# The token rows of k: transposed on VectorE in 32 by 32 blocks and stored in 128-byte runs by ScalarE, in place of TensorE transposes and a GpSimd store

## The chip, the core and the metric

The kernel runs on one core of a Trainium2 chip. The metric is device time in microseconds (us) for one execution; lower is better. Engines are TensorE (PE in the rows, its weight loads PEld), VectorE (DVE), ScalarE (ACT), GpSimd (POOL) and SyncE (SP). A transfer is requested by an engine's sequencer (SPq, ACTq, POOLq) and carried by 16 DMA engines that all requesters share.

## The reference, cut to what matters

One decoder layer is run on a group of 256 prompt tokens and a group of 8 samples with 4 tokens each, 288 tokens together. What matters here is that k leaves the kernel twice: inside, for attention, and as an output of its own with one row of 16 heads by 64 numbers per token.

```
h = _rmsnorm(x, g_pre) * (1.0 + scale) + shift
q, k, v, f, u, bg, cg, ga, gb = _split_cols(h @ w_in, IN_SIZES)
...
kp_l.append(k); vp_l.append(v)      # prompt: (256, 16, 64)
...
ks_l.append(k); vs_l.append(v)      # samples: (8, 4, 16, 64)
```

All numbers are float32. Every big product is made of three passes (high part by high part, and two cross terms).

## The kernel before, in words

Activations are kept transposed: a tile such as `kT` has 128 features on the partitions and, for each of 8 feature tiles, 288 tokens side by side. A product takes one megabyte of weights (`raw`, a ring of 4 buffers that SyncE fills), which ScalarE rounds to `w_hi` (L1327, `split_hi`) and VectorE turns to the remainder `w_lo` (L1794, `split_lo`), each in 2 buffers. TensorE then runs 48 matmuls (L675 to L677), in four column blocks of 12, numbered `mt` 0 to 3. `w_hi` of product n can be made only when product n-2 is done, since it uses the same buffer.

The stage around the change is the projection to q, k and v: a loop of 24 products, `u` = 0 to 23. I call them product 0 to 23. Products 0 to 11 make the first half of the features (q, k, v by four products each), 12 to 23 the second half. So `kT` is complete after product 19. Each engine has its own program, written out by hand; work is placed in it behind `if u == ...`, and semaphores join the engines. Nothing reorders it.

The token rows of k are made so. `turn_rows` has TensorE transpose four 128 by 128 tiles of `kT` into a PSUM bank (L951), 6 times for k and 6 times for v; ScalarE and VectorE take turns to copy the bank out (`copy_row`, L438) into `k_rows`, and GpSimd requests two stores of them (L2733, L2734). On TensorE two of the six stand behind product 19 and four behind product 21. Behind product 20 stands `turn_suf` (L943), 16 transposes for the bias of the samples; it waits for `cum_done`, which VectorE gives at the end of `copy_sums` (its last copies are L2183), and for the first two k row copies.

Behind product 21 ScalarE copies the four banks of `turn_suf` (L1505) and signals `sufT_done`. In product 23, the last, TensorE also transposes pages of the key cache (`turn_k`, L972): two ahead of `mt` 1 and two ahead of `mt` 2. The second pair uses the same banks as the first, and waits until ScalarE (`copy_KT`, L1489) and VectorE have copied them out. Ahead of that copy ScalarE does `new_keys` (L1493). In attention, ScalarE's `pair_hi(0)` (L1569) writes where `k_rows` lay, so it waits until the stores of k have landed (`s_kout`).

Of the kernel before, what the change touches and what calls it, by code (L numbers as in the profile page):

```python
# [67 lines left out]
def layer(nc, x_prompt, x_sample, cache_k, cache_v, cache_logf, state_conv, page_table, c_prompt,  # L68
# [86 lines left out]
    LAST = KT - 1  # L155
    H_HI = KT // PIECE

    ROWS = ([("k", half, b) for half in range(2) for b in range(3)]
            + [("v", 0, 0), ("v", 0, 1), ("v", 1, 0), ("v", 1, 1), ("v", 0, 2), ("v", 1, 2)])
    ROW_BANK = (4, 5, 4, 5, 6, 7, 6, 7, 2, 3, 7, 2)  # L160
    KEYS = PAST + TS
    CT = KA // 2

# [1 line left out]
    with ctx:  # L165
# [7 lines left out]
        def place(name, shape, dt=F32, where=None):  # L173
# [99 lines left out]
        k_rows = place("k_rows", [P, 3, DA], where=R)  # L273
# [102 lines left out]
        fixed, newk_ready, pool_sel, sums_ready = (sem(n) for n in ("fixed", "newk_ready", "pool_sel", "sums_ready"))  # L376
        z_ready, z_ps, z_out = sem("z_ready"), sem("z_ps"), sem("z_out")
        y_made = sem("y_made")
        rowT_ps, rowT_a, rowT_d, suf_ps, suf_done, sufT_ps, sufT_done = (sem(n) for n in (
            "rowT_ps", "rowT_a", "rowT_d", "suf_ps", "suf_done", "sufT_ps", "sufT_done"))  # L380

# [44 lines left out]
        def row_tile(n):  # L426

            name, half, b = ROWS[n]
            at_ = slice(512 * half, 512 * half + 512)
            if name == "k":  # L430
                return k_rows[0:min(P, NT - b * P), b, at_]
            return v_rows[half][:, b, :] if b < 2 else v_new[:, at_]

        def copy_row(eng, copy, n):
# [221 lines left out]
        def _(pe):  # L656
# [289 lines left out]
            def turn_rows(n):  # L946

                name, half, b = ROWS[n]
                rows = min(P, NT - b * P)
                for j in range(4):  # L950
                    mm = pe.transpose(bank[ROW_BANK[n]][0:rows, j * P:j * P + P],  # L951
                                      (kT if name == "k" else vT)[:, 4 * half + j, b * P:b * P + rows], ident[:, :])
                mm.then_inc(rowT_ps, 1)

            def turn_k(s, ns):
# [20 lines left out]
            def first_rows(mt):  # L976

                if mt == 1:
                    pe.wait_ge(rowT_a, 3)
                    pe.wait_ge(rowT_d, 3)  # L980
                    turn_k(0, (0, 1))
                if mt == 2:
                    turn_k(0, (2, 3))
                if mt == 3:
                    pe.wait_ge(bank_turn, BT + MT * (G_QKV + 4))
                    turn_rows(6)
                    turn_rows(7)

            for u in range(QKV):
                t = u % PER_HALF  # L990
                product(N_QKV + u, t % 4 == 0, t % 4 == 3, G_QKV + u // 4, SK * (t % 4), a_hi, a_lo, u % SPLIT,
                        None, first_rows if u == QKV - 1 else None)
                if u in ADA_AT:
                    v = 1 + ADA_AT.index(u)
                    pe.wait_ge(ada_turned, v)
                    ada_rows(v % SK, use=A_B1 + v + 1 - SPARE)
                if u == 0:
                    turn_z()
                if u == 3:
                    turn_lf()  # L1000
                if u == 19:
                    sums_of_lf()
                    pe.wait_ge(ada_turned, 1 + len(ADA_AT))
                    pe.wait_ge(ada_mods, A_B1 + 1)
                    pe.wait_ge(bank_turn, BT + MT * (G_QKV + 3))
                    turn_rows(0)
                    turn_rows(1)
                if u == 20:
                    turn_suf()
                if u == 21:  # L1010
                    pe.wait_ge(sufT_done, 1)
                    pe.wait_ge(bank_turn, BT + MT * (G_QKV + 6))
                    for n in range(2, 6):
                        turn_rows(n)

            def scores(s):

# [101 lines left out]
            scores(0)  # L1119
            pe.wait_ge(pool_sel, 1)  # L1120
            pe.wait_ge(sufT_done, 1)
            pe.wait_ge(rowT_a, 4)
            sample_scores(0)
            pe.wait_ge(bank_turn, BT + MT * (G_MIX + 1))
            turn_rows(8)
            turn_rows(9)
            pe.wait_ge(rowT_d, 4)
            turn_rows(10)
            pe.wait_ge(rowT_a, 5)
            turn_rows(11)  # L1130
            turn_k(1, (0, 1))
            scores(1)
            pe.wait_ge(rowT_a, 6)
            pe.wait_ge(rowT_d, 6)
            turn_p(0, 0)
            turn_p(0, 1)
            turn_k(1, (2, 3))
# [181 lines left out]
        def _(act):  # L1319
# [172 lines left out]
            def new_keys(j):  # L1492
                nc.scalar.copy(KTs[j][:, :, PAST:KEYS], kT[:, :, TP:NT]).then_inc(sK_new, 1)  # L1493

            for u in range(QKV):
                n = N_QKV + u
                if u < QKV - 1:
                    split_hi(n + 1, (u + 1) % RAW, (n + 1) // RAW + 1, (u + 1) % SPLIT)
                if u == 20:
                    copy_row(act, nc.scalar.copy, 0)  # L1500
                if u == 21:
                    act.wait_ge(sufT_ps, 1)
                    act.wait_ge(fixed, 1)
                    for b in range(4):
                        ins = nc.scalar.copy(bias_s[:, 2 * b:2 * b + 2, 0:PAST],  # L1505
                                             bank[4 + b][:, :].rearrange("p (s n) -> p s n", s=2))
                    ins.then_inc(sufT_done, 1)
                if u == 22:
                    copy_row(act, nc.scalar.copy, 2)
                    copy_row(act, nc.scalar.copy, 4)  # L1510
                if u == QKV - 1:
                    groups_done(N_QKV + u - 1, MT - 1)
                    new_keys(0)
                    copy_KT(0, 0)
                    evict(u, 0)
                    copy_KT(0, 2)
                    evict(u, 1)
                    copy_row(act, nc.scalar.copy, 6)
# [46 lines left out]
            def pair_hi(s):  # L1565
                act.wait_ge(O_ps, s + 1)
                if s == 0:
                    act.wait_ge(s_kout, 32)
                nc.scalar.copy(o_hi[:, s, 0:TP], bank[3][:, 0:TP]).then_inc(O_hi, 1)  # L1569

            def sample_hi(s):
# [6 lines left out]
                ins.then_inc(sO_hi, 1)  # L1578

            exp_head(0, 0)  # L1580
            copy_row(act, nc.scalar.copy, 8)
            copy_row(act, nc.scalar.copy, 10)
            exp_head(0, 1)
            exp_sample(0)
            act.wait_ge(rowT_ps, len(ROWS))
# [202 lines left out]
        def _(dve):  # L1788
# [398 lines left out]
            def copy_KT(s, n):  # L2187
# [54 lines left out]
            copy_row(dve, nc.vector.tensor_copy, 7)  # L2242

            def max_head(s, j):

# [55 lines left out]
            max_head(0, 0)  # L2301
            max_head(0, 1)
            max_sample(0)
            copy_row(dve, nc.vector.tensor_copy, 9)
            norm_head(0, 0)
            copy_row(dve, nc.vector.tensor_copy, 11)
            copy_KT(1, 1)
            norm_head(0, 1)
            max_head(1, 0)
# [336 lines left out]
        def _(pool):  # L2646
# [81 lines left out]

            pool.wait_ge(bank_turn, BT + MT * (G_QKV + 5))
            samples_q(0)  # L2730
            pool.wait_ge(rowT_a, 3)
# [3 lines left out]
            samples_q(1)  # L2735
            pool.wait_ge(rowT_a, 6)
            pool.wait_ge(rowT_d, 6)
# [11 lines left out]
            pool.wait_ge(s_kout, 32)  # L2749
            pool.wait_ge(s_zout, 32)  # L2750


# [56 lines left out]
```

## Time and profile before

| | us |
|---|---|
| median of 3 runs | 1783.26 (1783.14 to 1783.98) |
| the profiled execution | 1783.0 |
| its span in the trace | 1781.4 |
| TensorE busy in the span | 1768.5 |
| VectorE busy | 911.0 |
| ScalarE busy | 693.8 |
| the stage of this change (product 19's end to product 23's end) | 377.8 to 412.8 |

The profiled execution took 1.6 us more than its span; what lies around the span is not touched by the change. Times in the rows are us from the start of the span. Matmul rows overlap each other by their pipeline, so their start times tell the pace, not their durations.

### The profile page before, as it was taken

The page shows a single profiled execution, that of the slowest core. Times are in us where ns is not written, and L with a number is a line of the kernel's source. Part 1 is how long each engine was busy: PE and PEld are TensorE (multiplying, and loading weights), DVE is VectorE, ACT ScalarE, POOL GpSimd, SP SyncE. Part 2 cuts the span into 40 slices and gives each one's busy share as a digit, 9 for nine tenths or more (in the row PEclk, how much of TensorE's full clock was granted, in tenths as well). Part 3 has the DMA queues.
Part 4 walks back from the last instruction along what each step waited for, and adds up shares of the span by engine and source line. Part 5 has one row for each costly group of instructions (what it writes and reads, how often), then busy time and mean ns, then how long its engine had stood idle before and what let it go on. Part 6 is the DMA issues. An engine that isn't in the chain of part 4 may idle for free.

```text
span 1781.4 us, 31779 instructions
## 1 busy us (share of the span) xinstructions
PE 1768.5 (99%) x13592; PEld 1664.2 (93%) x13592; DVE 911.0 (51%) x1137; ACT 693.8 (39%) x809; POOL 26.1 (1%) x76
## 2 busy tenths in 40 slices
PE   8999999999999999999999999999999999999999
PEld 6888888897699999998979999999999999999998
DVE  4666663245644344455686444434443445566565
ACT  5332232235643333343354233333333334445454
POOL 0000100001000000000000000000000000000000
PEclk9999999999999999999999999999999999999999
DMA  9988578856754444458866444444444444444441
GB/s 380 409 333 336 214 309 343 355 200 223 262 185 165 163 159 167 162 196 343 332 245 265 142 166 165 165 165 165 165 165 165 165 163 166 164 163 164 163 161 71
DMA packets 59234, 382.38 MB, mean 215 GB/s; under 512 B 6912, under 2 KB 7728, under 8 KB 17026
## 3 DMA queue, kind: packets, MB, share of 16 engines
q1 hardware_dynamic: 57632, 378.27, 56.0%
q0 software_dynamic: 1328, 2.58, 0.4%
q8 instruction: 74, 1.21, 0.3%
q14 instruction: 22, 0.18, 0.0%
q10 hardware_dynamic: 178, 0.13, 0.0%
HBM read 376.15 MB, written 4.81 MB: 214 GB/s over the span
## 4 chain that ended last, share of the span: by engine, by line
PE 96%; DMA 1%; DVE 1%; ACT 1%; issue 1%; SPq 0%; DVEq 0%; ACTq 0%
PE bank L675 29%; PE bank L677 29%; PE bank L676 28%; PE bank L695 3%; PE bank L685 1%; PE bank L972 1%; DMA ada<-in_w_ada 1%; PE bank L1102 1%; PE bank L1071 0%; PE bank L1290 0%; DMA ada_o<-in_w_ada 0%; PE bank L1041 0%; PE bank L951 0%; PE bank L1051 0%; PE bank L898 0%
## 5 line engine op out<-in xcount | busy, mean ns | idle before, releaser
L675 PE MATMUL bank<-a_lo,w_hi 128*128 128x288 f32 x3624 | 1077.0, 297 | 1.4 <-DVE a_lo L1978 0.7
L676 PE MATMUL bank<-a_hi,w_hi 128*128 128x288 f32 x3624 | 1069.1, 295 | 0.0
L677 PE MATMUL bank<-a_hi,w_lo 128*128 128x288 f32 x3624 | 1065.5, 294 | 0.0
L1794 DVE TENSOR_TENSOR w_lo<-raw,w_hi 128x2048 fp32r<-128x2048 f32 x239 | 547.9, 2292 | 699.9 <-ACT w_hi L1327 699.2
L1327 ACT CAST w_hi<-raw 128x2048 fp32r<-128x2048 f32 x238 | 453.9, 1907 | 850.2 <-PE bank L677 824.7
L675 PEld LDWEIGHTS bank<-a_lo,w_hi 128*128 128x128 f32 x3624 | 678.9, 187 | 20.7 <-issue 19.2
L677 PEld LDWEIGHTS bank<-a_hi,w_lo 128*128 128x128 f32 x3624 | 682.6, 188 | 0.0
L676 PEld LDWEIGHTS bank<-a_hi,w_hi 128*128 128x128 f32 x3624 | 680.3, 188 | 0.0
L1906 DVE TENSOR_TENSOR a_lo<-hid,a_hi 128x1152 fp32r<-128x1152 f32 x44 | 59.4, 1351 | 12.3 <-ACT a_hi L1351 12.3
L1351 ACT CAST a_hi<-hid 128x1152 fp32r<-128x1152 f32 x44 | 50.7, 1154 | 0.0
L675 PE MATMUL bank<-o_lo,w_hi 128*128 128x288 f32 x128 | 37.9, 296 | 0.0
L675 PE MATMUL bank<-y_lo,w_hi 128*128 128x288 f32 x128 | 37.9, 296 | 0.0
L676 PE MATMUL bank<-o_hi,w_hi 128*128 128x288 f32 x128 | 37.8, 295 | 0.0
L676 PE MATMUL bank<-y_hi,w_hi 128*128 128x288 f32 x128 | 37.8, 295 | 0.0
L677 PE MATMUL bank<-o_hi,w_lo 128*128 128x288 f32 x128 | 37.6, 294 | 0.0
L677 PE MATMUL bank<-y_hi,w_lo 128*128 128x288 f32 x128 | 37.6, 294 | 0.0
L695 PE MATMUL bank<-ada,cT 128*32 128x512 f32 x288 | 32.8, 595 | 0.0
L1743 ACT ACTIVATE sg<-bank 128x288 f32<-128x288 f32 x44 | 18.0, 408 | 36.9 <-PE bank L677 36.9
L685 PE MATMUL bank<-ada,cT 128*32 128x512 f32 (+1 forms) x320 | 30.9, 512 | 0.6 <-DMA ada<-in_w_ada 0.6
L2578 DVE TENSOR_TENSOR sg<-bank,sg 128x288 f32<-128x288 f32 x44 | 19.0, 454 | 15.4 <-ACT sg L1743 15.4
L1663 ACT ACTIVATE sq<-bank 128x288 f32<-128x288 f32 x32 | 13.1, 409 | 32.5 <-PE bank L677 32.5
L695 PEld LDWEIGHTS bank<-ada,cT 128*32 128x32 f32 x288 | 8.4, 109 | 17.6 <-issue 17.6
(387 smaller groups left out, 973.4 us busy)
## 6 DMA issues: line engine op xcount, KB each, us to landing
raw<-in_w_ffn_in SPq DMA_DIRECT2D x88, 1024.0 KB, 4.8
raw<-in_w_in SPq DMA_DIRECT2D x75, 1024.0 KB, 7.9
ada<-in_w_ada SPq DMA_DIRECT2D x60, 1024.0 KB, 8.9
raw<-in_w_ffn_out SPq DMA_DIRECT2D x44, 1024.0 KB, 4.8
ada_o<-in_w_ada SPq DMA_DIRECT2D x24, 1024.0 KB, 8.4
raw<-in_w_o SPq DMA_DIRECT2D x16, 1024.0 KB, 4.9
ada<-in_w_ada SPq DMA_DIRECT2D x16, 512.0 KB, 12.6
raw<-in_cache_k SPq DMA_DIRECT2D x16, 512.0 KB, 4.2
```

The costliest lines, as they stand in the source:

```text
L675: pe.matmul(acc, w_hi[buf][:, a, cols], lo[:, kt, :], start=first and a == 0, stop=False)
L676: pe.matmul(acc, w_hi[buf][:, a, cols], hi[:, kt, :], start=False, stop=False)
L677: mm = pe.matmul(acc, w_lo[buf][:, a, cols], hi[:, kt, :], start=False, stop=last and a == tiles - 1)
L685: mm = pe.matmul(bank[4][32 * a:32 * a + 32, 0:src.shape[2]], cT[:, SK * q + a, :], src[:, a, :], start=q == 0, stop=q == SK - 1, tile_pos ...
L695: mm = pe.matmul(bank[4][32 * a:32 * a + 32, :], cT[:, k, :], ring[q][:, a, :], start=first and q == 0, stop=last and q == SK - 1, tile_po ...
L972: mm = pe.transpose(bank[4 + n % 2][:, f * P:f * P + P], raw[2 * j][:, n, f * P:f * P + P], ident[:, :])
L1327: nc.scalar.copy(w_hi[buf][:, :, :], raw[s][:, :, :]).then_inc(hi_done, 1)
L1351: nc.scalar.copy(dst[:, kd:kd + tiles, :], src[:, bass.ds(kt, tiles), :]).then_inc(act_hi, 1)
L1743: nc.scalar.activation(sg[:, mt, :], bank[mt][:, 0:NT], ACT.Sigmoid).then_inc(gate_done, 1)
L1794: tt(w_lo[buf][:, :, :], raw[s][:, :, :], w_hi[buf][:, :, :].bitcast(F32), ALU.subtract).then_inc(raw_turn, 1)
L1906: tt(lo[:, kd:kd + SK, :], src[:, bass.ds(kt, SK), :], hi[:, kd:kd + SK, :].bitcast(F32), ALU.subtract).then_inc(act_lo, 1)
L2578: tt(sg[:, mt, :], bank[mt][:, 0:NT], sg[:, mt, :], ALU.mult).then_inc(bank_turn, 1)
```

## The change

K's rows no longer pass through TensorE and PSUM. VectorE transposes `kT` in blocks of 32 by 32 from SBUF to SBUF, one instruction of 128 partitions by 1152 elements for each half of the features, into `k_blocks` (which lies where `k_rows` lay). In a block the tokens are now on 32 partitions and 32 features lie side by side, so a store writes runs of 32 numbers, 128 bytes. ScalarE requests the stores: for each half 16 of 32 partitions by 8 runs (the prompt) and 4 of 32 partitions by 4 runs (the samples), 20 requests; 40 in all. In the output each run stands alone, so there are 32 times 256 runs for the prompt and 8 times 128 for the samples, 9216. `turn_rows` and `copy_row` remain for v, with new numbers, and GpSimd keeps the stores of v.

```diff
-    ROWS = ([("k", half, b) for half in range(2) for b in range(3)]
-            + [("v", 0, 0), ...])
+    ROWS = ([("v", 0, 0), ("v", 0, 1), ("v", 1, 0), ("v", 1, 1), ("v", 0, 2), ("v", 1, 2)])
+    K_STORES = 4 * (KA + 2)
...
             def turn_suf():
                 pe.wait_ge(suf_done, 1)
                 pe.wait_ge(cum_done, 1)
-                pe.wait_ge(rowT_a, 1)
-                pe.wait_ge(rowT_d, 1)
+                pe.wait_ge(ada_turned, 1 + len(ADA_AT))
...
                 if mt == 1:
-                    pe.wait_ge(rowT_a, 3)
-                    pe.wait_ge(rowT_d, 3)
+                    pe.wait_ge(sufT_done, 1)
                     turn_k(0, (0, 1))
...
                 if u == 19:
                     sums_of_lf()
-                    turn_rows(0)
-                    turn_rows(1)
                 if u == 20:
                     turn_suf()
-                if u == 21:
-                    for n in range(2, 6):
-                        turn_rows(n)
...
+            def store_k(half):
+                tiles = slice(KA // 2 * half, KA // 2 * half + KA // 2)
+                prompt = k_prompt[0, 0].rearrange("(j r) (k x) (y c) -> x y r k j c", r=32, x=2, y=2)
+                sample = k_sample[0].rearrange("s t (k x) (y c) -> x y (s t) k c", x=2, y=2)
+                act.wait_ge(k_turned, half + 1)
+                for i in range(4):
+                    rows = slice(32 * i, 32 * i + 32)
+                    for k in range(KA // 2 * half, KA // 2 * half + KA // 2):
+                        act.dma_start(prompt[i // 2, i % 2, :, k, :, :],
+                                      k_blocks[rows, k, 0:TP].rearrange("p (j c) -> p j c", c=32)).then_inc(s_kout, 16)
+                    act.dma_start(sample[i // 2, i % 2, :, tiles, :], k_blocks[rows, tiles, TP:NT]).then_inc(s_kout, 16)
...
-                if u == 20:
-                    copy_row(act, nc.scalar.copy, 0)
                 if u == 21:
                     act.wait_ge(sufT_ps, 1)
...
                     ins.then_inc(sufT_done, 1)
+                    store_k(0)
                 if u == 22:
-                    copy_row(act, nc.scalar.copy, 2)
-                    copy_row(act, nc.scalar.copy, 4)
+                    store_k(1)
...
             def pair_hi(s):
                 act.wait_ge(O_ps, s + 1)
                 if s == 0:
-                    act.wait_ge(s_kout, 32)
+                    act.wait_ge(s_kout, 16 * K_STORES)
...
+            def turn_k_blocks(half):
+                dve.wait_ge(bank_turn, BT + MT * (G_QKV + 3 + 3 * half))
+                tiles = slice(KA // 2 * half, KA // 2 * half + KA // 2)
+                nc.vector.transpose(k_blocks[:, tiles, :].rearrange("p k n -> p (k n)"),
+                                    kT[:, tiles, :].rearrange("p k n -> p (k n)")).then_inc(k_turned, 1)
...
                 if u == 20:
                     copy_sums()
-                    copy_row(dve, nc.vector.tensor_copy, 1)
-                if u == 22:
-                    copy_row(dve, nc.vector.tensor_copy, 3)
-                    copy_row(dve, nc.vector.tensor_copy, 5)
+                    turn_k_blocks(0)
+                if u == 21:
+                    turn_k_blocks(1)
...
-            pool.dma_start(k_prompt[0, 0].rearrange("(b p) h d -> p b (h d)", p=P), k_rows[:, 0:2, :]).then_inc(s_kout, 16)
-            pool.dma_start(k_sample[0].rearrange("s t h d -> (s t) (h d)"), k_rows[0:TS, 2, :]).then_inc(s_kout, 16)
```

On ScalarE, from the `w_hi` of product 22 (the first row) to the first page copy of product 23, the program before reads:

```order
L1327 CAST w_hi_78<-raw_76 128x2048
L1505 COPY bias_s<-bank 128x2x256 x4
L1327 CAST w_hi_80<-raw_77 128x2048
L438 COPY k_rows<-bank 32x512
L438 COPY k_rows<-bank 128x512
L1493 COPY KTs_132<-kT 128x8x32
L1489 COPY KTs_132<-bank 128x4x128
```

The same stretch of ScalarE's program in the changed kernel, where the line numbers have shifted and each pair of rows of DMA requests is one quarter of a half:

```order
L1314 CAST w_hi_78<-raw_76 128x2048
L1503 COPY bias_s<-bank 128x2x256 x4
L1491 DMA out<-k_blocks 32x8x32 x4
L1493 DMA out<-k_blocks 32x4x32
...
L1314 CAST w_hi_80<-raw_77 128x2048
L1491 DMA out<-k_blocks 32x8x32 x4
L1493 DMA out<-k_blocks 32x4x32
...
L1480 COPY KTs_132<-kT 128x8x32
L1476 COPY KTs_132<-bank 128x4x128
```

The pair of request rows stands four times in each place: 20 requests now stand between the bias copies and the `w_hi` of product 23, and 20 between that and the page copy; two row copies have gone.

On VectorE, from the last copies of `copy_sums` to the page copies of product 23, the program before reads:

```order
L2183 COPY bias_s<-bank 128x4 x8
L438 COPY k_rows<-bank 128x512
L1794 TENSOR_TENSOR w_lo_79<-raw_76,w_hi_78 128x2048
L1794 TENSOR_TENSOR w_lo_81<-raw_77,w_hi_80 128x2048
L438 COPY k_rows<-bank 128x512
L438 COPY k_rows<-bank 32x512
L2197 COPY KTs_132<-bank 128x4x128 x2
```

And in the changed kernel:

```order
L2181 COPY bias_s<-bank 128x4 x8
L2202 STREAM_TRANSPOSE k_blocks<-kT 128x1152
L1792 TENSOR_TENSOR w_lo_79<-raw_76,w_hi_78 128x2048
L2202 STREAM_TRANSPOSE k_blocks<-kT 128x1152
L1792 TENSOR_TENSOR w_lo_81<-raw_77,w_hi_80 128x2048
L2195 COPY KTs_132<-bank 128x4x128 x2
```

One transpose now stands ahead of the `w_lo` of product 22 and one behind it; three row copies have gone.

## Rows read from the trace of the kernel before

**Rows 1.** The page: busy time by engine, and the chain by engine.

```profile
PE 1768.5 (99%) x13592; PEld 1664.2 (93%) x13592; DVE 911.0 (51%) x1137; ACT 693.8 (39%) x809; POOL 26.1 (1%) x76
...
PE 96%; DMA 1%; DVE 1%; ACT 1%; issue 1%; SPq 0%; DVEq 0%; ACTq 0%
```

**Rows 2.** Instructions of line 951: engine, operation, count, duration ns min/median/max.

```profile
L951 PE MATMUL bank<-ident,kT x24: 271/272/329, 379.6 to 397.3; 128*128 128x128 f32 x16, 128*32 128x128 f32 x8
```

**Rows 3.** Timeline of TensorE: start us, us, instruction, idle before and releaser.

```profile
387.46 1.94 PE L943 MATMUL bank<-ident,suf 128*128 128x128 f32 x16 [0.39 <-DVE k_rows L438]
...
395.63 1.91 PE L951 MATMUL bank<-ident,kT 128*32 128x128 f32 x16
397.30 0.38 PE L675 MATMUL bank<-a_lo,w_hi 128*128 128x288 f32 x1
```

**Rows 4.** Timeline of VectorE, products 20 to 22.

```profile
385.82 0.64 DVE L2183 COPY bias_s<-bank 128x4 f32<-128x4 f32 x8
386.62 0.69 DVE L438 COPY k_rows<-bank 128x512 f32<-128x512 f32 x1 [0.16 <-DVE bias_s L2183]
...
397.82 2.29 DVE L1794 TENSOR_TENSOR w_lo<-raw,w_hi 128x2048 fp32r<-128x2048 f32 x1 [6.43 <-ACT w_hi L1327]
```

**Rows 5.** Timeline of ScalarE, products 21 to 23.

```profile
387.16 1.90 ACT L1327 CAST w_hi<-raw 128x2048 fp32r<-128x2048 f32 x1 [6.30 <-PE bank L677]
389.44 2.05 ACT L1505 COPY bias_s<-bank 128x512 f32<-128x512 f32 x4 [0.37 <-PE bank L943]
395.88 1.90 ACT L1327 CAST w_hi<-raw 128x2048 fp32r<-128x2048 f32 x1 [4.39 <-PE bank L677]
...
403.97 0.41 ACT L1493 COPY KTs<-kT 128x256 f32<-128x256 f32 x1 [5.23 <-PE bank L677]
406.01 0.59 ACT L1489 COPY KTs<-bank 128x512 f32<-128x512 f32 x1 [1.63 <-PE bank L972]
```

**Rows 6.** Timeline of TensorE: product 23's start and its second pair of page transposes.

```profile
403.77 0.30 PE L675 MATMUL bank<-a_lo,w_hi 128*128 128x288 f32 x1
...
407.85 1.03 PE L972 MATMUL bank<-ident,raw 128*128 128x128 f32 x8
```

**Rows 7.** Instructions of tile ada_sb: VectorE's transpose of 128 by 512 out of PSUM.

```profile
L1886 DVE STREAM_TRANSPOSE ada_sb<-bank x14: 707/709/717, 199.4 to 1004.9; 128x512 f32<-128x512 f32 x14
```

**Rows 8.** Timeline of ScalarE and its queue: the three requests that it makes.

```profile
172.31 1.91 ACT L1327 CAST w_hi<-raw 128x2048 fp32r<-128x2048 f32 x1 [4.49 <-PE bank L677]
172.32 0.40 ACTq L1459 DMA_DIRECT2D bf<-in_b_f  x1
172.75 0.53 ACTq L1460 DMA_DIRECT2D table<-in_page_table  x1
173.31 0.36 ACTq L1461 DMA_DIRECT2D wf<-in_w_f  x1
```

**Rows 9.** Instructions of line 470: SyncE's weight requests, duration ns min/median/max.

```profile
L470 SPq DMA_DIRECT2D raw<-in_w_in x75: 327/333/1079, 42.1 to 741.9; - x75
```

**Rows 10.** Windows: busy us and count by engine, TensorE clock, DMA share, GB/s.

```profile
10.00:20.00 10.00, 9.46 (x96) 6.49 (x98) 4.56 (x17) 5.45 (x12) 0.00 (x0) 1.00 1.03 414
...
1775.00:1777.00 2.00, 2.00 (x21) 2.00 (x20) 1.88 (x4) 1.30 (x3) 0.00 (x0) 1.00 1.02 366
...
391.00:409.00 18.00, 18.00 (x143) 17.88 (x143) 4.64 (x6) 5.15 (x10) 1.25 (x2) 1.00 0.50 183
```

**Rows 11.** The page: ScalarE's DMA queue, packets, MB, share of 16 engines.

```profile
q10 hardware_dynamic: 178, 0.13, 0.0%
```

**Rows 12.** Timeline of ScalarE: the copy that waits for the landed k stores.

```profile
422.21 0.35 ACT L1569 CAST o_hi<-bank 128x256 fp32r<-128x256 f32 x1
```

**Rows 13.** Timeline of SyncE's queue: a request near the start, and key pages of sample 1.

```profile
9.37 1.75 SPq L499 DMA_DIRECT2D raw<-in_w_in  x1
...
391.56 0.85 SPq L579 DMA_DIRECT2D raw<-in_cache_k  x2
```

**Rows 14.** The chain in order of time: transposes of the key pages of sample 1.

```profile
417.31 0.87 PE bank L972 x8
```

More of the change, by code:

```diff
@@ L156, in layer @@
     H_HI = KT // PIECE
-    ROWS = ([("k", half, b) for half in range(2) for b in range(3)]
-            + [("v", 0, 0), ("v", 0, 1), ("v", 1, 0), ("v", 1, 1), ("v", 0, 2), ("v", 1, 2)])
-    ROW_BANK = (4, 5, 4, 5, 6, 7, 6, 7, 2, 3, 7, 2)
+    ROWS = ([("v", 0, 0), ("v", 0, 1), ("v", 1, 0), ("v", 1, 1), ("v", 0, 2), ("v", 1, 2)])
+    ROW_BANK = (6, 7, 2, 3, 7, 2)
+    K_STORES = 4 * (KA + 2)
     KEYS = PAST + TS
@@ L272, in layer @@
         o_lo = place("o_lo", [P, KA, NT], F32R, where=R + B_ACT8)
-        k_rows = place("k_rows", [P, 3, DA], where=R)
+        k_blocks = place("k_blocks", [P, KA, NT], where=R)
         upto = place("upto", [P, TP], where=R + 3 * DA * 4)
@@ L378, in layer @@
         y_made = sem("y_made")
+        k_turned = sem("k_turned")
         rowT_ps, rowT_a, rowT_d, suf_ps, suf_done, sufT_ps, sufT_done = (sem(n) for n in (
@@ L429, in row_tile @@
             at_ = slice(512 * half, 512 * half + 512)
-            if name == "k":
-                return k_rows[0:min(P, NT - b * P), b, at_]
             return v_rows[half][:, b, :] if b < 2 else v_new[:, at_]
@@ L951, in turn_rows @@
                     mm = pe.transpose(bank[ROW_BANK[n]][0:rows, j * P:j * P + P],
-                                      (kT if name == "k" else vT)[:, 4 * half + j, b * P:b * P + rows], ident[:, :])
+                                      vT[:, 4 * half + j, b * P:b * P + rows], ident[:, :])
                 mm.then_inc(rowT_ps, 1)
@@ L985, in first_rows @@
                     pe.wait_ge(bank_turn, BT + MT * (G_QKV + 4))
-                    turn_rows(6)
-                    turn_rows(7)
+                    turn_rows(0)
+                    turn_rows(1)
             for u in range(QKV):
@@ L1121, in _ @@
             pe.wait_ge(sufT_done, 1)
-            pe.wait_ge(rowT_a, 4)
+            pe.wait_ge(rowT_a, 1)
             sample_scores(0)
             pe.wait_ge(bank_turn, BT + MT * (G_MIX + 1))
[L1125 to L1130, printed above, removed]
+            turn_rows(2)
+            turn_rows(3)
+            pe.wait_ge(rowT_d, 1)
+            turn_rows(4)
+            pe.wait_ge(rowT_a, 2)
+            turn_rows(5)
             turn_k(1, (0, 1))
             scores(1)
-            pe.wait_ge(rowT_a, 6)
-            pe.wait_ge(rowT_d, 6)
+            pe.wait_ge(rowT_a, 3)
+            pe.wait_ge(rowT_d, 3)
             turn_p(0, 0)
@@ L1517, in _ @@
                     evict(u, 1)
-                    copy_row(act, nc.scalar.copy, 6)
+                    copy_row(act, nc.scalar.copy, 0)
                     evict(u, 2)
@@ L1580, in _ @@
             exp_head(0, 0)
-            copy_row(act, nc.scalar.copy, 8)
-            copy_row(act, nc.scalar.copy, 10)
+            copy_row(act, nc.scalar.copy, 2)
+            copy_row(act, nc.scalar.copy, 4)
             exp_head(0, 1)
@@ L2235, in _ @@
                     copy_sums()
-                    copy_row(dve, nc.vector.tensor_copy, 1)
-                if u == 22:
-                    copy_row(dve, nc.vector.tensor_copy, 3)
-                    copy_row(dve, nc.vector.tensor_copy, 5)
+                    turn_k_blocks(0)
+                if u == 21:
+                    turn_k_blocks(1)
             copy_KT(0, 1)
             copy_KT(0, 3)
-            copy_row(dve, nc.vector.tensor_copy, 7)
+            copy_row(dve, nc.vector.tensor_copy, 1)
             def max_head(s, j):
@@ L2303, in _ @@
             max_sample(0)
-            copy_row(dve, nc.vector.tensor_copy, 9)
+            copy_row(dve, nc.vector.tensor_copy, 3)
             norm_head(0, 0)
-            copy_row(dve, nc.vector.tensor_copy, 11)
+            copy_row(dve, nc.vector.tensor_copy, 5)
             copy_KT(1, 1)
@@ L2730, in _ @@
             samples_q(0)
+            samples_q(1)
             pool.wait_ge(rowT_a, 3)
             pool.wait_ge(rowT_d, 3)
-            pool.dma_start(k_prompt[0, 0].rearrange("(b p) h d -> p b (h d)", p=P), k_rows[:, 0:2, :]).then_inc(s_kout, 16)
-            pool.dma_start(k_sample[0].rearrange("s t h d -> (s t) (h d)"), k_rows[0:TS, 2, :]).then_inc(s_kout, 16)
-            samples_q(1)
-            pool.wait_ge(rowT_a, 6)
-            pool.wait_ge(rowT_d, 6)
             for half in range(2):
@@ L2748, in _ @@
             pool.wait_ge(s_out, 16 * 6)
-            pool.wait_ge(s_kout, 32)
+            pool.wait_ge(s_kout, 16 * K_STORES)
             pool.wait_ge(s_zout, 32)
```

5 lines of the change are left out of this document (removed).

## The prediction

> **What bounds the kernel now.** I read the page first. TensorE is busy for 1768.5 of 1781.4 us and holds 96% of the chain that ended last [rows 1]. So time is saved only by what leaves TensorE's own sequence, and lost by whatever makes TensorE wait. Next I read the timelines of the three compute engines around the change, to see who waits for whom there. TensorE runs without a gap, except for 0.39 us ahead of the transposes of `turn_suf`, where it waits for VectorE's k row copy [rows 3]. ScalarE is idle most of this stage: 4.39 us ahead of the `w_hi` of product 23 and 5.23 us ahead of `new_keys` [rows 5]. The change spends those two gaps.
>
> **What TensorE sheds.** 24 transposes leave [rows 2]. Eight stood behind product 19; taking them away only lets product 20 end sooner, and then `turn_suf` waits for VectorE. It started at 387.46, 0.15 us after the k row copy (386.62 + 0.69 = 387.31) [rows 3, 4]. Without that copy it follows the end of `copy_sums`, 385.82 + 0.64 = 386.46, by a signal and the same 0.15, some 386.7: **0.76 us sooner**. The other sixteen filled 395.63 to 397.30 [rows 3]: **1.67 us**, and some 0.1 for the slower first matmul behind a transpose (0.38 against 0.30) [rows 3, 6]. Together TensorE can gain at most 2.5 us. Undisturbed, product 21 would end at 395.63 - 0.76 = 394.87, product 23 would start at 403.77 - 2.5 = 401.27, and its second page transposes, in the trace at 407.85 [rows 6], would start at 405.35. I use this start as the mark: behind it TensorE's program is as before, so what the mark moves, the end moves.
>
> **What VectorE takes on.** Two transposes of 1152 elements. The nearest row is 709 ns for 512 elements out of PSUM [rows 7]; in proportion 1.6 us each. The first starts at about 386.6, ends at 388.2, and stands ahead of the `w_lo` of product 22. That one cannot start before its `w_hi`, which in the trace ends at 387.16 + 1.90 = 389.06 [rows 5]; with product 20 ending up to 0.9 sooner, 388.2. So the first costs nothing, and product 22 needs its `w_lo` only at 394.87. The second runs in VectorE's idle 6.43 us ahead of the `w_lo` of product 23 [rows 4]. If the transpose cost twice as much, 3.2 us, `w_lo` of product 22 would end at 389.8 + 2.3 = 392.1, still in time. Cost 0. The row copies that leave both engines were in gaps too.
>
> **What ScalarE takes on.** This decides. A sequencer makes requests one after the other, and each one behind them waits. Let c be the time from one request to the next. The nearest rows are ScalarE's own three requests: 0.40, 0.53 and 0.36 us, and from 172.32 to 173.67 the three take 1.35 us, so c = 0.45 [rows 8]. SyncE's repeated requests have 0.333 us at the median [rows 9], with the 0.03 us between neighbours c = 0.36. Upward, one request of the group at the start took 1.75 us [rows 13], which I come to below. I take 0.45: it is the same queue. The same rows show that requests run while the cast that stands ahead of them (172.31, 1.91 us) is still under way, so the casts and copies ahead do not add to them.
>
> - The bias copies start 0.76 sooner, at 388.68, and the last of the four is begun some 1.5 us later, at 390.2. There the first 20 requests start, and `k_turned` has come by then. They end at 390.2 + 20c = 399.2.
> - Only then can the `w_hi` of product 23 start, in the trace at 395.88. From its start to the end of `w_lo` are 397.82 + 2.29 - 395.88 = 4.23 us [rows 4, 5]. Product 23 can start at 394.5 + 20c = 403.5, not at 401.27: TensorE stands 2.2 us. The mark, 4.08 us behind that start [rows 6], would be 398.6 + 20c = 407.6.
> - The next 20 requests run beside the cast and end at 390.2 + 40c = 408.2. Behind them wait `new_keys` (0.3 until the next) and the page copy (0.59) [rows 5], on which TensorE's second page transposes wait. So the mark cannot be sooner than 391.15 + 40c = **409.15**.
>
> The later of the two counts, the second for every c over 0.373. The mark moves by 409.15 - 407.85 = **+1.3 us**; in general by 40c - 16.7. Every 0.01 us of a request is worth 0.4 us of the kernel. With c = 0.36 the first bound holds, 398.6 + 7.2 = 405.8, and the kernel is 2.05 us faster; with c = 0.53, the longest of the three, it is 4.5 us slower.
>
> **Free, with its cover.** The landing: `pair_hi(0)` is at 422.21 [rows 12] and needs all stores; with the last request at 408.2 it has 14 us, more by the shift. The page loads: those of sample 1 are requested at 391.56 [rows 13] and used at 417.31 [rows 14], 25 us. GpSimd loses two requests that nobody waits for.
>
> **The runs of 128 bytes.** Each DMA engine gets 16 + 1 runs of a prompt store (256 over 16, and the signal) and 8 + 1 of a sample store: 32 x 17 + 8 x 9 = 616 in all. Let t be the time of one. Rows of 8 KB went at 414 GB/s [rows 10], 317 ns per row and engine; the output rows of 2 KB at 366 GB/s, 90 ns. A straight line through both gives 14 ns for a row and 4.7 for 128 bytes, so t = 18.5 ns as a lower estimate; it was read off far larger rows. The upper bound is ScalarE's queue itself: its share rounds to 0.0%, so under 0.05% of 16 x 1781.4 us, 14 us for 178 packets, 80 ns each [rows 11]. The DMA engines were busy 50% of 391 to 409, with the store of k in it (1.15 MB at the 366 GB/s, 3.2 us of 18); so loads take 32% and 68% is free. 616 x 18.5 ns = 11.4 us, over 0.68 = 16.8 us, just under the 18 us that 40 requests take. I take it as hidden, from the nearest figure, but by little.
>
> That a full queue holds its requester up is what the 1.75 us request shows: it was made at 9.37, when the DMA engines were at their full rate [rows 10, 13], and a neighbour without that load takes 0.33.
>
> A rule speaks against the change. The Trainium skill, "DMA: Bandwidth & Descriptors", section Specifications, says that a transfer needs 512 bytes or more for full rate and that below this a read-modify-write is done. No row of this trace shows stores of single short runs, so it neither agrees nor differs; by the rule the stores would come out as the third rival below, by the straight line as hidden.
>
> **The rivals.** *All is covered* (chance 0.10): requests cost what SyncE's repeated ones cost, c = 0.36 or less. For it: all 32 prompt requests have one shape and tensor. Against: ScalarE's own rows. -2 to -2.5 us, 1780.5 to 1781.
>
> *The queue fills* (0.23): t is 25 to 40 ns, and ScalarE can request only as fast as the runs drain. Leaving out some 60 runs per engine that may still stand in the queue at the end (an estimate: ahead of the slow request at 9.37 some six requests of 9 packets were open), the requests end at 390.2 + 556t/0.68, that is 20 us after for t = 25 and 33 for t = 40, and the mark moves by +4 to +16 us: 1787 to 1799. It takes over from the count of requests at t = 22 ns and passes 0.2% at 25, near the estimate.
>
> *Short runs are stored in two passes* (0.13): a run is first read and then written, and costs near the upper bound, 60 to 80 ns. 556 x 60 / 0.68 = 49 us and 65 us; the mark at 440 and 457, +32 to +48 us, 1815 to 1831. Against it: 80 is a bound, not a reading. This is the mechanism of the page's rule; its 512 bytes twice, at the straight line's 33 ns each, would be an estimate of 66 ns and 1820.
>
> *The requests themselves are dearer* (0.10): with three dimensions and 256 runs, twice the runs of any in the trace, c = 0.53 to 0.60. +4.5 to +7.3 us, 1787.5 to 1790.3. For it: the spread of 0.36 to 0.53 between simple ones.
>
> That the transposes do not leave is excluded by the order of the programs. A gain over 0.2% would need more than the 2.5 us that TensorE sheds; I leave 0.02 for what I overlook.
>
> **The numbers.** The profiled execution took 1783.0, its span 1781.4; the median of the runs is 1783.26. Forecast (chance 0.42): 1783.0 + 1.3 = 1784.3, its own range 1781 to 1786.6. What a measurement can tell from no change is 0.2%, 3.6 us. Same: 0.42 + 0.10 = 0.52. Slower: 0.23 + 0.13 + 0.10 = 0.46. Faster 0.02. The range reaches from all covered, 1780.5, to the upper end of the filled queue, 1799, and leaves out the two passes and some of the rest, under 2 in 10.
>
> **What would show it.** Right: 40 request rows of ScalarE's queue of about 0.42 us each; the second L972 of product 23 (L970 now) at about 409, with its idle time put down to ScalarE's page copy; product 23 starting at about 403.5 after 2 us of idle; `turn_suf` at 386.7; two VectorE transposes of 1.2 to 1.6 us. Wrong: requests that start at 0.4 and grow to 0.6 or more after the first few (the queue fills), or a `pair_hi(0)` that waits for a DMA. If the requests have 0.33 the gain of TensorE is kept. The forecast is wrong at once if c is over 0.507, where +3.6 us is passed.

## The result, and the profile after

The changed kernel took 1786.88 us (median of 18 runs, 1785.60 to 1788.68), the kernel before 1783.30 us on the same chip (18 runs, of which one took 9829 us; without that one the median is 1783.26). The ratio is 1.002, with a 95% interval of 1.0014 to 1.0026: 3.6 us slower. The forecast was 1784.3, with a range of 1780.5 to 1799. So the sign was right and the time lies in the range, but the loss is 2.6 us larger than the sum, which gave 1.0 to the median, and the time is 0.3 us above the range of 1781 to 1786.6 that belonged to this sum alone. The profiled execution took 1788.5 us, the second longest of its 18. Its stage also began 1.41 us later than in the trace of before, ahead of anything that the change touches. The last matmul that both programs share ahead of it (`bank<-upto,lfr`) starts at 378.83 in before and at 380.24 here (near the start of the trace TensorE waited 1.4 us for `in_x_sample` and 1.2 us for `ada_o`, against 0.2 and 0.7 before). I therefore take 1.41 from each time of after before I set it beside [rows 3 to 6].

The page of the changed kernel: busy times, the queue of ScalarE, the shares of the chain that ended last, and the largest group of TensorE, whose last column is its idle time and what ended it.

```profile
PE 1769.7 (99%) x13568; PEld 1665.5 (93%) x13568; DVE 911.6 (51%) x1136; ACT 692.3 (39%) x806; POOL 24.9 (1%) x74
...
q10 hardware_dynamic: 10034, 1.31, 0.4%
...
PE 96%; ACT 1%; DVE 1%; DMA 1%; ACTq 1%; issue 0%; SPq 0%; DVEq 0%
...
L674 PE MATMUL bank<-a_lo,w_hi 128*128 128x288 f32 x3624 | 1078.1, 297 | 4.4 <-DVE w_lo L1792 3.0
```

TensorE is busy 1.2 us *more* than before [rows 1], though 24 transposes left it. ACTq, ScalarE's requests, now stands in the chain with 1%. And one wait of 3.0 us for `w_lo` is new.

ScalarE's timeline in the stage, which answers to [rows 5]; ACTq rows are requests, a row with x4 holds four in sequence:

```profile
390.00 0.59 ACT L1503 COPY bias_s<-bank 128x512 f32<-128x512 f32 x1 [0.36 <-PE bank L941]
390.02 0.86 ACTq L1491 DMA_DIRECT2D out<-k_blocks  x2
...
390.90 1.51 ACTq L1491 DMA_DIRECT2D out<-k_blocks  x1
...
396.43 1.99 ACTq L1491 DMA_DIRECT2D out<-k_blocks  x4
...
400.94 0.47 ACTq L1493 DMA_DIRECT2D out<-k_blocks  x1
401.51 1.91 ACT L1314 CAST w_hi<-raw 128x2048 fp32r<-128x2048 f32 x1 [9.45 <-PE bank L676]
401.53 1.87 ACTq L1491 DMA_DIRECT2D out<-k_blocks  x4
...
411.33 0.47 ACTq L1493 DMA_DIRECT2D out<-k_blocks  x1
411.84 0.41 ACT L1480 COPY KTs<-kT 128x256 f32<-128x256 f32 x1 [8.43 <-issue]
412.15 0.58 ACT L1476 COPY KTs<-bank 128x512 f32<-128x512 f32 x1
```

The first 20 requests run from 390.02 to 401.41, and the cast of product 23 starts only behind them. The profile writes its idle time to TensorE (`PE bank L676`). The requests beside the gap show what it is: ScalarE's own sequencer was making requests throughout. The second 20 run beside the cast, to 411.80, and behind them stand `new_keys` (L1480) and the page copy (L1476).

TensorE's timeline behind product 22, which answers to [rows 6]:

```profile
405.79 0.61 PE L674 MATMUL bank<-a_lo,w_hi 128*128 128x288 f32 x1 [3.03 <-DVE w_lo L1792]
406.20 0.44 PE L675 MATMUL bank<-a_hi,w_hi 128*128 128x288 f32 x1
406.44 0.44 PE L676 MATMUL bank<-a_hi,w_lo 128*128 128x288 f32 x1
...
408.84 1.91 PE L970 MATMUL bank<-ident,raw 128*128 128x128 f32 x8
...
412.08 0.29 PE L676 MATMUL bank<-a_hi,w_lo 128*128 128x288 f32 x1
412.21 0.29 PE L674 MATMUL bank<-a_lo,w_hi 128*128 128x288 f32 x1
```

The windows of TensorE over the same stretch (length, busy time and count, granted clock, DMA share, GB/s):

```profile
400.00:402.00 2.00, 2.00 (x17) 1.00 0.41 66
402.00:404.00 2.00, 0.76 (x6) 1.00 0.37 58
404.00:406.00 2.00, 0.21 (x1) 0.69 0.37 58
406.00:408.00 2.00, 2.00 (x9) 0.50 0.66 112
408.00:410.00 2.00, 2.00 (x11) 0.50 0.98 377
```

Behind the idle 3.03 us the matmuls start 0.24 us apart in place of 0.13, and the granted clock is 0.50, that is 1.2 GHz. Such a slow engine counts as fully busy: from the shared matmul to the mark TensorE is busy 29.12 us where it was 28.63, +0.5 us in spite of the 2.5 us that left it. The other 0.7 us of the 1.2 lie ahead of the shared matmul and have nothing to do with the change. The mark, the second page transposes, starts at 412.79. Counted from the shared matmul that is 32.55 us, against 407.85 - 378.83 = 29.02 before: +3.53 us. That is nearly all of the difference of the medians, 3.58. (The two profiled executions lie 5.5 us apart: 1.41 ahead of the shared matmul, 3.53 here, and 0.56 behind the mark.) It starts just behind ScalarE's page copy (412.15 + 0.58 = 412.73).

### The profile page after: what moved, and what is told of

It reads as the page before. It is cut to its first block, busy times and chain, and to the rows that moved or that the text cites. A ratio compares the mean times of both kernels' runs of the same rounds, so it can differ in the third digit from the quotient of the medians.

```text
span 1786.9 us, 31761 instructions
## 1 busy us (share of the span) xinstructions
PE 1769.7 (99%) x13568; PEld 1665.5 (93%) x13568; DVE 911.6 (51%) x1136; ACT 692.3 (39%) x806; POOL 24.9 (1%) x74
## 3 DMA queue, kind: packets, MB, share of 16 engines
q10 hardware_dynamic: 10034, 1.31, 0.4%
## 4 chain that ended last, share of the span: by engine, by line
PE 96%; ACT 1%; DVE 1%; DMA 1%; ACTq 1%; issue 0%; SPq 0%; DVEq 0%
PE bank L674 29%; PE bank L676 28%; PE bank L675 28%; PE bank L694 3%; PE bank L684 2%; PE bank L970 1%; PE bank L1089 1%; PE bank L1058 0%; ACTq L1491 0%; DMA ada_o<-in_w_ada 0%; PE bank L1277 0%; DMA xs_rows<-in_x_sample 0%; PE bank L1028 0%; PE bank L731 0%; DVE w_lo L1792 0%
## 5 line engine op out<-in xcount | busy, mean ns | idle before, releaser
L676 PE MATMUL bank<-a_hi,w_lo 128*128 128x288 f32 x3624 | 1066.2, 294 | 0.0
L676 PEld LDWEIGHTS bank<-a_hi,w_lo 128*128 128x128 f32 x3624 | 683.3, 189 | 0.0
L676 PE MATMUL bank<-o_hi,w_lo 128*128 128x288 f32 x128 | 37.6, 294 | 0.0
L676 PE MATMUL bank<-y_hi,w_lo 128*128 128x288 f32 x128 | 37.6, 294 | 0.0
```

Source lines behind the costliest of these rows:

```text
L676: mm = pe.matmul(acc, w_lo[buf][:, a, cols], hi[:, kt, :], start=False, stop=last and a == tiles - 1)
```

## The experiments

Each experiment is an edit of the changed kernel. Medians are set against runs of the kernel before on the same chip: 1783.22 for the first four, 1782.95 for the other four. "The mark" is always counted from the same shared matmul, so +3.53 is that of the change.

**No stores.** What does TensorE gain when nobody makes the requests?

```diff
-                    store_k(0)
-                if u == 22:
-                    store_k(1)
...
-                    act.wait_ge(s_kout, 16 * K_STORES)
+                    act.wait_ge(k_turned, 2)
...
-            pool.wait_ge(s_kout, 16 * K_STORES)
```

> The changed kernel without any store of k (k_prompt and k_sample are left unwritten; VectorE still makes the blocks). Theory 1, requests: ScalarE's 40 requests are the whole loss, and without them only what TensorE shed is left: 2.5 us under the kernel before, 1780.8 us, the second pair of page transposes 2.5 us sooner than in the kernel before, and no idle time of TensorE between products 22 and 23. Rival: part of the 3.6 us comes from something else in the change (VectorE's transposes, GpSimd's order, the added waits); then this kernel stays above 1781.5.

Measured: 1780.31 us, ratio 0.9987 (0.9978 to 0.9996), 2.9 us faster; the mark moved by -2.59. So the removed transposes give what the sum said, 2.5 within 0.1, and VectorE's transposes cost nothing. The change loses all of that and 3.6 us more by its stores alone.

**Runs of 1 KB.** The same 32 prompt requests with the same bytes, but each writes 32 long runs in place of 256 short ones.

```diff
-                        act.dma_start(prompt[i // 2, i % 2, :, k, :, :],
-                                      k_blocks[rows, k, 0:TP].rearrange("p (j c) -> p j c", c=32)).then_inc(s_kout, 16)
+                        act.dma_start(wide[i, k, :, :], k_blocks[rows, k, 0:TP]).then_inc(s_kout, 16)
```

> The changed kernel with the 32 prompt requests storing 1 KB runs (2 per engine and request instead of 16) at wrong places of k_prompt; same number of requests, same bytes. Theory 1, the request itself costs about 0.47 to 0.5 us whatever its runs: the 40 requests still take 20 us, and the kernel stays at +2 to +4 us against the kernel before. Theory 2, the queue of short runs holds the requests up (one took 1.51 us in the changed kernel): the requests fall to 0.36 to 0.42 us, none is longer than 0.6, and the kernel is at -1.5 to +0.5 us.

Measured: 1785.11 us, ratio 1.0011 (1.0002 to 1.0020), 1.9 us slower than before, just under the first theory's +2 to +4; mark +1.58. The prompt requests of the changed kernel, then those of this one (minimum, median and maximum in ns, first and last start):

```profile
L1491 ACTq DMA_DIRECT2D out<-k_blocks x32: 356/473/1506, 390.0 to 410.8; - x32
```

```profile
L1491 ACTq DMA_DIRECT2D out<-k_blocks x32: 339/444/1115, 390.3 to 409.1; - x32
```

With an eighth of the runs the median request falls by only 0.03 us and the 40 together from 21.8 to 19.9 us. So most of the price belongs to the request itself, not to its runs. Of the 1.9 us between them 0.03 x 40 = 1.2 are the shorter requests and 0.4 the one long request. TensorE's two waits here, and three windows of the kernel:

```profile
404.95 0.40 PE L674 MATMUL bank<-a_lo,w_hi 128*128 128x288 f32 x1 [1.87 <-DVE w_lo L1791]
411.16 1.09 PE L970 MATMUL bank<-ident,raw 128*128 128x128 f32 x8 [1.88 <-ACT KTs L1476]
```

```profile
400.00:402.00 2.00, 2.00 (x18) 1.00 0.24 57
404.00:406.00 2.00, 1.05 (x8) 1.00 0.28 68
412.00:414.00 2.00, 2.00 (x18) 1.00 0.29 63
```

After 1.87 us of idle the clock stayed at 1.00 (the second window), and after the next 1.88 us too (the third). With it TensorE is early enough to be seen waiting for ScalarE's page copy, the bound that the sum named. In the changed kernel the slow clock covers that wait.

The windows also price the short runs for the DMA engines. They are busy 0.41 of the time at 66 GB/s with runs of 128 bytes, 0.24 at 57 GB/s with 1 KB. The Trainium skill ("DMA: Bandwidth & Descriptors", section Specifications) wants 512 bytes for full rate and has a read-modify-write below that. The trace agrees that short runs cost more for each byte, 1.5 times by these two windows. It does not show the 60 to 80 ns per run that the prediction's rival of two passes needed: ScalarE's queue was 0.4% busy, 0.004 x 16 x 1786.9 = 114 us over 10034 packets, some 11 ns each (10 to 13 by the rounding).

**Half by SyncE.** ScalarE keeps the first 20 requests, SyncE takes the second 20. This takes the page copy out from behind requests and leaves the delayed cast.

```diff
+            load_pages(1, 0)
+            store_k(1, sp)
+            load_pages(1, 1)
...
-                if u == 22:
-                    store_k(1)
```

> The changed kernel with the first 20 requests by ScalarE as before and the second 20 by SyncE, behind its request for the key pages of sample 1. Now ScalarE's page copy is free, and only the late w_hi of product 23 is left: product 23 starts about 0.6 us later than in the kernel before, behind 3 us of idle. Theory A, the idle costs its own length and no more: second page transposes 4.08 us behind that start, +0.6 us, 1783.9. Theory B, TensorE comes out of the idle at half its clock, as the changed kernel's rows show (0.24 us per matmul instead of 0.133), and the price is the slow stretch too: +2.5 to +3.5 us, hardly better than the changed kernel.

Measured: 1786.32 us, ratio 1.0019 (1.0010 to 1.0028), 3.1 us slower; mark +2.60. TensorE's row of product 23, and its windows:

```profile
404.44 0.40 PE L689 MATMUL bank<-a_lo,w_hi 128*128 128x288 f32 x1 [3.35 <-DVE w_lo L1805]
...
405.34 0.45 PE L690 MATMUL bank<-a_hi,w_hi 128*128 128x288 f32 x1
```

```profile
404.00:406.00 2.00, 1.56 (x7) 0.69 0.19 45
406.00:408.00 2.00, 2.00 (x11) 0.50 0.92 367
```

Nothing of ScalarE stands ahead of the mark now, and yet little is won. From the start of product 23 to the mark it is 10.19 - 4.44 = 5.75 us where it was 4.08 at full clock [rows 6]: the slow clock costs 1.7 us here. So the change is held by two bounds that lie near each other, ScalarE's second 20 requests and TensorE's own slow stretch, and taking the first away alone gives only 3.53 - 2.60 = 0.9 us of mark.

**All by SyncE.** The same with both halves, behind the request of the first pages of sample 1.

```diff
+            load_pages(1, 0)
+            store_k(0, sp)
+            store_k(1, sp)
+            load_pages(1, 1)
```

> All 40 requests by SyncE, behind its request for the key pages of sample 1 and ahead of those for the value pages of sample 1; ScalarE makes none. Theory 1, who requests is what costs: 2.5 us under the kernel before, 1780.8 us, as without stores. Theory 2, the short runs or the later page requests hold something up (the requests take about 18 us, so the value pages come 10 us later than before): the gain is smaller than without stores, by what TensorE or pair_hi(0) waits for a DMA; 1782 to 1786.

Measured: 1780.32 us, ratio 0.9989 (0.9980 to 0.9998), 2.9 us faster by the medians and 2.0 by the ratio; mark -2.58, as without any store. The requests as SyncE's queue made them:

```profile
L591 SPq DMA_DIRECT2D out<-k_blocks x32: 316/450/487, 391.3 to 411.8; - x32
```

They cost SyncE nearly what they cost ScalarE, 0.45 us, and up to the mark they cost the kernel nothing. Behind them wait the page loads. The value pages of sample 1 are requested at 414.0 and nobody waits for them, but the key pages of sample 2 follow at 416.25. That is 37.7 us behind the shared matmul, against 27.6 in the kernel without stores, whose row is this:

```profile
406.13 14.32 SPq L578 DMA_DIRECT2D raw<-in_cache_k  x4
```

Here TensorE stands for these pages, and the clock falls behind that wait:

```profile
416.25 4.29 SPq L578 DMA_DIRECT2D raw<-in_cache_k  x4
...
426.43 1.09 PE L986 MATMUL bank<-ident,raw 128*128 128x128 f32 x8 [2.22 <-DMA raw<-in_cache_k]
```

```profile
428.00:430.00 2.00, 2.00 (x10) 0.50 0.84 342
```

From the mark to a matmul behind this place (the fourth `bank<-ncum,pick` behind the mark, at 432.88) it is 27.90 us, against 24.15 without stores (404.92 to 429.07): 3.75 us lost, 2.22 of them by standing and 1.5 behind it. This profiled execution took 1783.93 us, the longest of eleven. The eleven fall into two groups, six of 1779.54 to 1780.32 us and five of 1782.23 to 1783.93 us, while all eleven without stores stay under 1781.5. So the second theory holds in at least one execution: the median of 1780.32 is that of the executions without the loss, and SyncE is not a free place for these requests. Only one execution was profiled, so that the other four lost their time to the same wait is likely but not shown.

**The clock kept up.** To the half-by-SyncE kernel I add dummy matmuls in the idle stretch of TensorE, ahead of product 23. They wait for `sufT_done`, that is until ScalarE has copied the banks of `turn_suf`. That was long ago when product 22 ends, so they begin right behind it.

```diff
+                if u == 22:
+                    pe.wait_ge(sufT_done, 1)
+                    keep_warm(6, bank[7])
```

> e3_half_by_act with six dummy matmuls (128 by 128 by 256, into a free bank, some 0.46 us each, together 2.8 us) on TensorE between products 22 and 23, where it stood idle for 3.35 us. Theory B of e3 (the idle halves TensorE's clock and the slow stretch is most of the price): the clock stays at 1.00, matmuls keep 0.133 us, the second page transposes start 4.08 us behind product 23, 2 us sooner than in e3: 1784.0 to 1784.6. Rival (the slow pace comes from the DMA traffic or from something else in that stretch): it stays at 1786.3.

Measured: 1784.42 us, ratio 1.0007 (0.9998 to 1.0016), 1.5 us over before in place of 3.1; mark +0.76 in place of +2.60.

```profile
401.13 2.75 PE L728 MATMUL bank<-ones 128*128 128x256 f32 x12
...
404.38 0.40 PE L689 MATMUL bank<-a_lo,w_hi 128*128 128x288 f32 x1 [0.49 <-DVE w_lo L1808]
```

```profile
406.00:408.00 2.00, 2.00 (x18) 1.00 0.96 363
```

Product 23 starts nearly where it does in the kernel without them (0.27 us sooner from the shared matmul), but at granted clock 1.00, and from there to the mark it is 408.56 - 404.38 = 4.18 us in place of 5.75. So the clock's price is 1.6 us. The medians give 3.10 - 1.47 = 1.6 too, but each of them is known to 1.6 us only, so it is the traces that show it. The DMA engines move as much in the window of 406 to 408 as without the dummies (363 and 367 GB/s), so the traffic does not make the slow pace.

**The clock kept up in the changed kernel.** The same lines in the changed kernel itself.

> The changed kernel with the same six dummy matmuls. Here ScalarE's page copy behind all 40 requests holds the second page transposes as well, until about the same moment as the slow clock did. So the clock stays at 1.00 and nothing is gained, or at most 0.3 us: 1786.5 to 1787; TensorE's slow stretch turns into a wait for the page copy of some 2 to 3 us. Rival: the slow clock is what set the time, and the kernel gains 1.5 us or more.

Measured: 1788.08 us (7 runs), ratio 1.0027 (1.0016 to 1.0039), 5.1 us over before; the mark +3.57, where the change has it. I had expected no change of time, and it became 1.5 us slower. TensorE's rows, and its windows:

```profile
403.83 0.40 PE L674 MATMUL bank<-a_lo,w_hi 128*128 128x288 f32 x1 [0.16 <-DVE w_lo L1795]
...
411.16 1.55 PE L970 MATMUL bank<-ident,raw 128*128 128x128 f32 x8 [3.00 <-ACT KTs L1479]
412.75 0.44 PE L675 MATMUL bank<-a_hi,w_hi 128*128 128x288 f32 x1
```

```profile
410.00:412.00 2.00, 0.84 (x6) 0.91 0.16 26
412.00:414.00 2.00, 2.00 (x11) 0.50 0.11 29
```

The mark is held by ScalarE, as expected. But the fast product 23 now arrives 3.00 us early and waits there, the clock falls *behind* the mark, and there nothing covers the slow matmuls: from the mark to the fourth `bank<-ncum,pick` it is 25.77 us (411.16 to 436.93), against 24.22 in the changed kernel (412.79 to 437.01), 1.55 us more. In the changed kernel the slow stretch lay in time that TensorE would have waited anyway.

**Second half by ScalarE.** The mirror of the third experiment: SyncE makes the first 20 requests, ScalarE the second.

```diff
+            load_pages(1, 0)
+            store_k(0, sp)
+            load_pages(1, 1)
...
-                    store_k(0)
                 if u == 22:
```

> The first 20 requests by SyncE, the second 20 by ScalarE, behind the w_hi of product 23, which is now in time (394.75 in the time of e4). 20 requests of 0.51 us end at about 405.0, the page copy at 405.9, so the second page transposes start 0.9 to 1.3 us later than with all requests by SyncE (404.98): 1.2 to 1.7 us under the kernel before's mark. 1781.2 to 1781.9. Rival (two queues that request short runs at a time slow each other to 0.6 us and more): the mark comes 3 us late or more, 1783 to 1785.

Measured: 1781.88 us, ratio 0.9992 (0.9983 to 1.0001), 1.1 us under before; mark -1.33.

```profile
L1506 ACTq DMA_DIRECT2D out<-k_blocks x16: 410/474/484, 395.6 to 404.5; - x16
```

```profile
407.01 1.09 PE L985 MATMUL bank<-ident,raw 128*128 128x128 f32 x8 [1.10 <-ACT KTs L1491]
```

Twenty requests take 395.56 to 406.02, 10.46 us, and hold the page copy by 1.10 us. Product 23 starts in time and the clock stays up. The first twenty do the larger harm (3.1 us slower with them alone, 1.1 us faster with the second alone), since the cast hangs on them, and on the cast product 23 and the clock.

**All by GpSimd.** The 40 requests between GpSimd's two gatherings of q, in place of ScalarE's.

```diff
             samples_q(0)
+            store_k(0, pool)
+            store_k(1, pool)
             samples_q(1)
```

> All 40 requests by GpSimd, which stands idle from 370 on, ahead of samples_q(1) and the stores of v. Theory 1 (only the requester counts): GpSimd takes 0.51 to 0.75 us per request, so 40 take 21 to 30 us from 391, to 412 to 421. samples_q(1) is wanted at about 412 and pair_hi(0) at 419.5, so it comes out between the kernel with SyncE's requests and 3 us above it: 1780.5 to 1783.5. Rival: GpSimd writes descriptors for 256 runs per request and takes over 1 us each; then samples_q(1) is 20 us late and the kernel is slower than 1790.

Measured: 1780.17 us, ratio 0.9984 (0.9975 to 0.9993), 2.8 us faster; mark -2.58. It came 0.3 us under the range that I had given it. A request costs GpSimd more than the others, and the 40 take 23 us:

```profile
L2727 POOL DMA_DIRECT2D out<-k_blocks x32: 582/582/623, 388.4 to 410.1; - x32
```

Nobody waits: `samples_q(1)` starts at 412.89, when q is there. All eleven executions lie between 1779.74 and 1780.97 us, and SyncE, whose queue is free again, asks for the key pages of sample 2 at 406.59, 27.65 us behind the shared matmul, as without stores. This version computes all that the reference does, and each of its executions beats each of both kernels; by the medians it is 2.8 us faster than before and some 6.4 faster than the change.

## Why the prediction was right, and where its sum was short

- **TensorE sheds at most 2.5 us.** Right. `turn_suf` starts 388.03 - 380.24 = 7.79 us behind the shared matmul against 8.63 before [rows 3], 0.84 sooner where I had 0.76. Without the stores the mark moved by -2.59.
- **VectorE's transposes cost nothing.** Right. They took 1.375 us each in place of 1.6, and no row waits for them:

```profile
388.03 1.38 DVE L2202 STREAM_TRANSPOSE k_blocks<-kT 128x1152 f32<-128x1152 f32 x1 [0.16 <-DVE bias_s L2181]
389.68 2.29 DVE L1792 TENSOR_TENSOR w_lo<-raw,w_hi 128x2048 fp32r<-128x2048 f32 x1 [0.27 <-ACT w_hi L1314]
391.88 1.37 DVE L2202 STREAM_TRANSPOSE k_blocks<-kT 128x1152 f32<-128x1152 f32 x1
403.45 2.29 DVE L1792 TENSOR_TENSOR w_lo<-raw,w_hi 128x2048 fp32r<-128x2048 f32 x1 [10.19 <-ACT w_hi L1314]
```

- **The first 20 requests start at 390.2, when the last bias copy is begun.** Wrong, in the kernel's favour. They start with the first of the four copies, at 390.02 - 1.41 = 388.61: **1.6 us sooner**. [rows 8] had shown requests beside a running cast; that three more copies may stand ahead as well I had not taken from it.
- **c = 0.45 us.** The term that was too small. The 40 requests took 411.80 - 390.02 = 21.78 us, 0.545 each. By the formula 40c - 16.7 the mark would move by **3.8 us more** than at 0.45. Of these, 2.0 are the ordinary request (0.473 and the gap to the next, 0.50 in all), and 1.0 is one request of 1.51 us, the third. The rest is spread over a few of 0.56 to 0.67. The two errors together: 1.3 - 1.6 + 3.8 = +3.5, and the trace has +3.53. I had named c over 0.507 as the point at which the forecast is wrong. It was 0.545, which by the formula is +5.1 us; only the early start, which I had not foreseen, took that back to 3.58 us, where I had put the limit of "same" at 3.6. So the mechanism was right, and that the forecast of no change held is luck.
- **Both bounds were named rightly.** The cast waits for the first 20 and product 23 for it; from the cast's start to the end of `w_lo` are 405.74 - 401.51 = 4.23 us, as worked out. The page copy waits for all 40, and the mark stands behind it.
- **TensorE stands 2.2 us.** It stood 3.03, and a step was missing: the granted clock falls to 0.50 behind it. In the sum this changes little, since the page copy held the mark almost as long. TensorE alone could have started it at 412.48 + 0.13 = 412.61. It decides what a remedy is worth, as the half-by-SyncE kernel shows: 1.6 us of its 3.1 are the clock.
- **The rival of dearer requests (0.10)** came nearest to what happened: +4.5 us for c = 0.53, against +3.6. Its reason, that more runs make a request dearer, holds for about half: of the 3.8 us that the 40 requests took beyond 0.45 each, runs of 1 KB save 1.9 (21.8 to 19.9), 0.4 of them in the one long request. The rest is there with 32 runs as well.
- **The queue fills (0.23), two passes (0.13).** Both fell. A run took some 11 ns, less than my lower estimate of 18.5, and requests late in the sequence are no longer than early ones (0.50 apart in 396.43 to 398.42). The first 20 average 0.57 and the second 0.51, the reverse of a queue that fills.
- **The landing is free.** Right: `pair_hi(0)` (L1567) starts without a wait at 427.22, 15 us behind the last request.
- **All covered (0.10)** needed 0.36 for a request. No requester had that at the median.

**Open.** Why the third request is long: 1.51 us in the change, 1.11 with 1 KB runs, 1.10 to 1.45 in the three others where ScalarE makes the first twenty; never where it makes only the second twenty. SyncE, making all 40, had one of 1.92 us, but that was its thirtieth. No run tells its cause. And marks and medians differ by up to 0.7 us (+0.76 and +1.5 with the dummy matmuls in the half-by-SyncE kernel), about what the profiled execution and a median may differ by. Only where time is lost behind the mark, as with all requests by SyncE and with the clock kept up in the changed kernel, does the mark not tell the end: there my premise that the end moves as the mark does is wrong.

## What to carry to other kernels

Count requests, not bytes: a store cut into 40 requests holds the queue that makes them for 20 us, and each instruction behind them waits, even where the data would take a third of that. So put requests on a sequencer behind which nothing urgent stands. The same 40 cost 6.5 us of kernel on ScalarE and none on GpSimd; on SyncE they delay the page loads behind them, and the execution that was profiled lost 3.75 us by it. Look at every execution and not only at the median: it hid this. And where TensorE comes to stand for 2 or 3 us, price the slow clock behind it too, but fill the gap only where the filled time is not spent waiting at the next one.

## What the hardware showed that I had not expected

- ScalarE's requests ran ahead of copies that stood before them in its program. The first was made 0.02 us behind the start of the first of four copies (390.02 and 390.00). In the other direction no row here passes: the cast started 0.10 us behind the end of the twentieth request.
- A request costs by requester: 0.47 us at the median on ScalarE, 0.45 on SyncE, 0.58 on GpSimd, for the same 256 runs. The Trainium skill ("DMA: Bandwidth & Descriptors", section "Issuing engines are not separate DMA queues") calls the sequencer's time to initiate a transfer "usually small relative to the DMA itself". For one request that agrees: 0.47 us against 2.1 us at the median from request to landing. For 40 in a row it does not: 21.8 us of requests for 616 runs per DMA engine, which at 11 ns are 6.8 us.
- TensorE idle for 1.87, 1.88, 1.10 or 0.49 us was followed by a granted clock of 1.00. Idle for 3.03, 3.35, 3.00 or, with all requests by SyncE, 2.22 us it was followed by 0.50, which lasted up to 5.7 us (405.79 to 411.5) and cost 1.6 us where nothing else held the kernel.
